# A two-block transformer kernel: state-space stage reordered, lag shifts on ScalarE's queue, E tables and a shared product on GpSimd

## The chip, the cores and the metric

The kernel runs on one core of a Trainium2 chip. The metric is the device time of one execution in microseconds, as the median of several; lower is better.

## The reference, cut to what matters

The input x is [512, 1024]. A first block has two layers: a state-space mixer (S5) and a latent attention, each followed by a SwiGLU feed-forward. A second block has two layers of three kinds of attention. The change touches only the S5 mixer:

```python
u = (h @ w_in).reshape(bsz, seq, SSM_GROUPS, SSM_GROUP)      # 64 groups of 16 channels
decay = exp(lam_re * step); a = decay * (cos(lam_im * step), sin(lam_im * step))   # 64 complex states a group
b = f(a) * (b_re, b_im)
x_t = a * x_(t-1) + b u_t;   y_t = Re(c x_t) + d_skip * u_t
z = gelu(y)
val, gate = split(z @ w_glu); out = val * sigmoid(gate)
```

## The kernel before

Every large product is exact in float32 by splitting both operands into a high and a low part (float32r): three matmuls for each 128x128 tile of weights. ScalarE makes the high part of a weight block (`wh`, line 645), VectorE the low part (`wl`, line 1203), two blocks ahead of TensorE (`split_high`, `split_low`, called through `ahead` and `next_block`). The blocks come in one stream over the whole kernel, through four slots of `raw` that SyncE's queue fills (`load`, line 411) once a slot has been split. All semaphores count upwards, so a count names a block or a turn.

**The state-space stage.** The sequence of 512 is cut into NCH = 64 chunks of CH = 8 steps. Inside a chunk the recurrence is a small lower triangular (Toeplitz) matrix over 8 steps; between chunks it is a scan. The 64 groups go through in NQ = 4 turns q of 16 groups (QP = 8 pairs). Tables come first: the powers of a (`pw`), the gained powers (`pf`), and E (`Er`, `Ei`, [128, 32 pairs, 64 chunks]), the phases of a^8 raised to the chunk's number, by doubling. Er and Ei are made on GpSimd up to 32 columns (lines 534 to 541). For the last doubling (columns 32 to 63) GpSimd makes Er (lines 546 to 548) and VectorE Ei (`last_phases`, line 1350).

For each turn q:

- `make_g(q)` (VectorE, five operations of 1024 columns): G, the input matrices. The first operation is the product `ps * br` into `tv`; it is used by two later ones.
- `from_g(q, hs)` (TensorE): transposes G into banks 4 and 5; `copy_w` (ScalarE) copies them to WM.
- `lags(q)` (TensorE, line 2030): the lag matrix of G and C; `copy_lags` (ScalarE, line 707) copies it to the last row block of MS; seven DMAs on SyncE's queue (`mat_shift`, line 451) shift it into the other seven. The rest of MS is zero from a GpSimd memset (line 558).
- `states(q)` (TensorE, line 2046): the input of the scan for each chunk, from U[q % 2] and WM. Its completion is z_made.
- VectorE rotates this by E (six operations), scans (line 1438, two scans, with the decay rows `rho` that ScalarE fills in `decay_rows`), rotates back and writes `state` (six operations): s_ready.
- `outputs(q)` (TensorE, line 2061): Toeplitz part from MS and U: toeplitz_used. `state_outputs(q)` (line 2072): adds the part of `state` through the V tables of `make_v(q)` (GpSimd, five operations of 1024 columns): y_ready.
- ScalarE applies Gelu (line 782), TensorE turns the result (`turn_z`, line 2082), ScalarE and VectorE write its high and low part to zH and zL (`turned_high`, line 760, `turned_low`, line 1417), the input of w_glu.

The order on TensorE is written out by hand. Eight products of w_in fill the first part (n = 0 to 7), with from_g(0) and lags(0) behind n = 4 and states(0) ahead of n = 7. Then from_g(1), lags(1), outputs(0), states(1), state_outputs(0); then a turn for q = 1, 2, 3 of from_g(q+1, first half), turn_z(q-1), from_g(q+1, second half), lags(q+1), outputs(q), states(q+1), state_outputs(q). In the last turn parts of the first two w_glu blocks (`glu_part`) stand in place of lags.

`take_input(j)` (VectorE, line 1375) scales product j of w_in into T; SyncE's queue writes it to u_dram (line 456) and reads it back in another layout to U (`read_u`, line 443, eight DMAs a turn). read_u(1) waits for the writes of all of u; read_u(2) and read_u(3) wait for y_ready(1) and (2), behind mat_shift of the turn.

The queues before: VectorE goes take_input(4), last_phases, take_input(5), block 5's split, make_g(1), take_input(6), block 6's split, take_input(7), then the turns q. In turn q it goes rotation, turned_low(q-1), scans, rotation back, state, make_g(q+2); behind q = 0's state also block 7's split (blocks 6 and 7 here are the splits made ahead for the first two w_glu blocks). GpSimd goes E, make_v(0), a wait for all of u, memsets of rho, state and MS, make_v(1), make_v(2) after y_ready(1), make_v(3). ScalarE goes splits, WM copies, a wait for the memsets, copy_lags(0), WM copies, decay_rows(0) and (1), then the turns.

## Time and profile before

| | |
|---|---|
| median of 3 runs | 1895.33 us (1894.39 to 1896.41) |
| profiled execution, its own time | 1895.86 us |
| span of its core, first to last instruction | 1894.1 us |
| mean granted clock of TensorE | 0.982 of 2.4 GHz |
| TensorE busy | 1825.6 us, 96% |
| VectorE, ScalarE, GpSimd busy | 1051.8, 834.4, 191.8 us |

PE is TensorE, PEld its weight loads, DVE VectorE, ACT ScalarE, POOL GpSimd, SPq SyncE's queue (DVEq: a semaphore increment on VectorE's queue). The span is the time between the first and the last instruction that the profiler recorded. Busy shares are averages over stages with different limits. The page's slices, of 47 us each, show where TensorE is not full:

```profile
PE   7789999999999999999999999989999999999997
DVE  8594454444433767766444434466464566555647
ACT  5132344344222666744444422233466633356753
POOL 7950000000000000000000000023000102200000
PEclk9779999999999999999999999999999999999999
```

Each digit is the busy share of one fortieth of the span in tenths; the last line is the granted clock of TensorE in tenths. The first four slices hold w_in and the state-space stage.

### The profile page before, as it was taken

The page shows a single profiled execution, that of the slowest core. Times are in us where ns is not written, and L with a number is a line of the kernel's source. Part 1 is how long each engine was busy: PE and PEld are TensorE (multiplying, and loading weights), DVE is VectorE, ACT ScalarE, POOL GpSimd, SP SyncE. Part 2 cuts the span into 40 slices and gives each one's busy share as a digit, 9 for nine tenths or more (in the row PEclk, how much of TensorE's full clock was granted, in tenths as well). Part 3 has the DMA queues.
Part 4 walks back from the last instruction along what each step waited for, and adds up shares of the span by engine and source line. Part 5 has one row for each costly group of instructions (what it writes and reads, how often), then busy time and mean ns, then how long its engine had stood idle before and what let it go on. Part 6 is the DMA issues. An engine that isn't in the chain of part 4 may idle for free.

```text
span 1894.1 us, 24279 instructions
## 1 busy us (share of the span) xinstructions
PE 1825.6 (96%) x8908; PEld 1415.8 (75%) x8908; DVE 1051.8 (56%) x1622; ACT 834.4 (44%) x1400; POOL 191.8 (10%) x261
## 2 busy tenths in 40 slices
PE   7789999999999999999999999989999999999997
PEld 5677878888888766667888888868766777866675
DVE  8594454444433767766444434466464566555647
ACT  5132344344222666744444422233466633356753
POOL 7950000000000000000000000023000102200000
PEclk9779999999999999999999999999999999999999
DMA  6212223222333210112322333323111122311111
GB/s 217 74 38 72 89 90 100 99 91 98 92 99 99 70 34 27 61 57 89 100 92 96 100 92 92 106 74 106 67 56 49 53 78 85 105 56 56 55 41 61
DMA packets 58763, 152.19 MB, mean 80 GB/s; under 512 B 17152, under 2 KB 22048, under 8 KB 58672
## 3 DMA queue, kind: packets, MB, share of 16 engines
q1 hardware_dynamic: 55120, 148.27, 24.5%
q0 software_dynamic: 3552, 2.70, 0.5%
q8 instruction: 58, 0.95, 0.2%
q14 instruction: 33, 0.27, 0.0%
HBM read 143.79 MB, written 4.19 MB: 78 GB/s over the span
## 4 chain that ended last, share of the span: by engine, by line
PE 86%; POOL 4%; DVE 3%; ACT 3%; issue 1%; SPq 1%; DMA 0%; DVEq 0%; ACTq 0%; POOLq 0%
PE bank L1974 18%; PE bank L1975 18%; PE bank L1976 18%; PE bank L2462 3%; PE bank L2464 3%; PE bank L2463 3%; PE bank L2439 2%; PE bank L2427 2%; PE bank L2426 2%; PE bank L2425 2%; PE bank L2194 1%; PE bank L2222 1%; PE bank L2549 1%; PE bank L2477 1%; PE bank L2446 1%
## 5 line engine op out<-in xcount | busy, mean ns | idle before, releaser
L1203 DVE TENSOR_TENSOR wl<-raw,wh 128x1024 fp32r<-128x1024 f32 (+3 forms) x280 | 323.6, 1156 | 495.1 <-ACT wh L645 492.0
L645 ACT ACTIVATE wh<-raw 128x1024 fp32r<-128x1024 f32 (+3 forms) x280 | 279.1, 997 | 592.8 <-PE bank L1976 516.8
L1974 PE MATMUL bank<-xH,wh 128*128 128x512 f32 x904 | 355.9, 394 | 12.5 <-DVE wl L1203 10.6
L1975 PE MATMUL bank<-xL,wh 128*128 128x512 f32 x904 | 353.1, 391 | 0.0
L1976 PE MATMUL bank<-xH,wl 128*128 128x512 f32 x904 | 353.0, 390 | 0.0
L1974 PEld LDWEIGHTS bank<-xH,wh 128*128 128x128 f32 x904 | 170.6, 189 | 51.1 <-DVE wl L1203 10.2
L1975 PEld LDWEIGHTS bank<-xL,wh 128*128 128x128 f32 x904 | 170.6, 189 | 35.8 <-issue 1.0
L1976 PEld LDWEIGHTS bank<-xH,wl 128*128 128x128 f32 x904 | 170.4, 188 | 35.8
L1974 PE MATMUL bank<-hidH,wh 128*128 128x512 f32 x352 | 137.4, 390 | 0.0
L1975 PE MATMUL bank<-hidL,wh 128*128 128x512 f32 x352 | 137.0, 389 | 0.0
L1976 PE MATMUL bank<-hidH,wl 128*128 128x512 f32 x352 | 137.0, 389 | 0.0
L2462 PE MATMUL bank<-xH,wh 128*128 128x512 f32 x256 | 108.4, 424 | 0.0
L2464 PE MATMUL bank<-xH,wl 128*128 128x512 f32 x256 | 100.8, 394 | 0.0
L2463 PE MATMUL bank<-xL,wh 128*128 128x512 f32 x256 | 100.3, 392 | 0.0
L581 POOL TENSOR_TENSOR xT<-xT,acc 128x512 f32<-128x512 f32 x9 | 11.2, 1272 | 737.0 <-ACT acc L1003 737.0
L1872 DVE TENSOR_REDUCE least<-bank 128x1 f32<-128x128 f32 (+3 forms) x96 | 42.6, 485 | 73.5 <-PE bank L2446 73.4
L1059 ACT ACTIVATE Pm<-bank,least 128x128 f32<-128x128 f32 (+3 forms) x96 | 49.8, 523 | 68.4 <-DVE least L1872 68.4
L1975 PEld LDWEIGHTS bank<-hidL,wh 128*128 128x128 f32 x352 | 66.1, 188 | 13.9 <-issue 0.2
L1974 PEld LDWEIGHTS bank<-hidH,wh 128*128 128x128 f32 x352 | 66.1, 188 | 13.9 <-issue 0.2
L1976 PEld LDWEIGHTS bank<-hidH,wl 128*128 128x128 f32 x352 | 66.1, 188 | 13.7
L811 ACT ACTIVATE hidH<-T 128x512 f32 (+1 forms) x44 | 27.8, 632 | 78.3 <-DVEq L1488 78.3
L571 POOL COPY xT<-T 128x512 f32<-128x512 f32 x8 | 8.9, 1107 | 475.8 <-DVE T L1506 475.8
(449 smaller groups left out, 3335.8 us busy)
## 6 DMA issues: line engine op xcount, KB each, us to landing
raw<-w_gu_dram SPq DMA_DIRECT2D x88, 512.0 KB, 3.3
raw<-w_p_dram SPq DMA_DIRECT2D x64, 512.0 KB, 3.3
raw<-w_dn_dram SPq DMA_DIRECT2D x32, 448.0 KB, 3.3
raw<-w_glu_dram SPq DMA_DIRECT2D x16, 512.0 KB, 3.6
raw<-w_dn_dram SPq DMA_DIRECT2D x16, 512.0 KB, 3.5
raw<-w_out_dram SPq DMA_DIRECT2D x16, 512.0 KB, 3.3
raw<-w_in_dram SPq DMA_DIRECT2D x8, 512.0 KB, 7.8
raw<-w_o_dram SPq DMA_DIRECT2D x8, 512.0 KB, 3.2
```

What stands on the lines that cost most here:

```text
L645: nc.scalar.activation(wh[:, (st.base + u) % 2, 0:kts * P], raw[:, (st.base + u) % 4, 0:kts * P], ACT.Copy).then_inc(w_high, 1)
L1059: nc.scalar.activation(Pm[side][:, POFF[j]:POFF[j] + w], banks[side][:, 0:w], ACT.Exp, scale=-1.0, bias=least[:, j, side:side + 1], accum_ ...
L1203: nc.vector.tensor_tensor(wl[:, s, 0:kts * P], raw[:, (st.base + u) % 4, 0:kts * P], wh[:, s, 0:kts * P].bitcast(F32), ALU.subtract).then_ ...
L1872: nc.vector.tensor_reduce(least[:, j, side:side + 1], banks[side][:, 0:(j + 1) * P], AX, ALU.min)\
L1974: nc.tensor.matmul(bank, wh[:, s, w], hi[:, k, :], start=first and kt == 0, stop=False)
L1975: nc.tensor.matmul(bank, wh[:, s, w], lo[:, k, :], start=False, stop=False)
L1976: ins = nc.tensor.matmul(bank, wl[:, s, w], hi[:, k, :], start=False, stop=last and kt == kts - 1)
L2425: nc.tensor.matmul(o, xH[:, k, rows], wh[:, s, w], start=k == 0, stop=False)
L2426: nc.tensor.matmul(o, xH[:, k, rows], wl[:, s, w], start=False, stop=False)
L2462: nc.tensor.matmul(bank, wh[:, s, w], xH[:, kt, :], start=kt == 0, stop=False)
L2463: nc.tensor.matmul(bank, wh[:, s, w], xL[:, kt, :], start=False, stop=False)
L2464: ins = nc.tensor.matmul(bank, wl[:, s, w], xH[:, kt, :], start=False, stop=kt == KD - 1)
```

## The change

- VectorE's `last_phases` is removed; GpSimd makes both Er and Ei of the last doubling.
- GpSimd makes the product `ps * br` of make_g for q = 2 and 3 (`make_t`), into two new buffers in the space of xH and xL, which is free only once w_in is done. make_t(2) stands behind make_v(0) and a wait for the last write of u, make_t(3) behind make_v(1).
- GpSimd's three memsets are removed: rho and state are now set on VectorE behind take_input(7) in turn 0, MS by an activation of ScalarE.
- The seven shift DMAs are issued by ScalarE's queue, in copy_lags. SyncE's queue issues read_u(q+2) once outputs(q) is done (toeplitz_used) and not after state_outputs(q).
- rotr and roti lie in `tv` now.
- ScalarE: behind block 6 the order is WM copies (0, 1) of q = 1, decay_rows(0), WM copies (2, 3), MS zeroed, copy_lags(0), decay_rows(1), block 7's split.
- VectorE: make_g(1) stands behind take_input(4), take_input(7) behind the rotation of turn 0; turned_low(q-1) behind the scans; the splits of blocks 6 and 7 behind turn 2's state.
- TensorE: five matmuls on a buffer of small constants before the first product; from_g(1, (0, 1)) and then states(0) ahead of n = 7, the other half behind it; lags(1) no longer waits for lag_ready(1).

```diff
--- before.py
+++ after.py
@@ -248,13 +248,13 @@
     pf = late.tensor("pf", [P, 3, CH, NPAIR])
     C2 = Region(nc, late.base + 4 * KB, 4 * KB).tensor("C2", [P, 2, 2, QP, 2, GK])
     core = Region(nc, shared.base, 32 * KB)
-    rotr = core.tensor("rotr", [P, QP, NCH])
-    roti = core.tensor("roti", [P, QP, NCH])
+    rotr, roti = (tv[:, ri * QP * NCH:(ri + 1) * QP * NCH].rearrange("p (a b) -> p a b", a=QP) for ri in range(2))
     rho = core.tensor("rho", [P, 2, QP, NCH])
     state = core.tensor("state", [P, 2, QP, NCH])
     zs = core.tensor("zs", [P, 2, CH, 4, GK])
     MS = core.tensor("MS", [P, CH, QG, GK])
     VM1 = [zL_mem.tensor("VM1r", [P, QP, P]), zH_mem.tensor("VM1i", [P, QP, P])]
+    shared_t = [core.tensor(f"shared_t{q}", [P, QP * CH * GK]) for q in range(2)]
     VM3 = [T[:, 2:4, :].rearrange("p a (b c) -> p (a b) c", c=P), core.tensor("VM3i", [P, QP, P])]
     skip_rows = zH_mem.tensor("skip_rows", [GK, NG, GK])
     U = [U0, u_mem.tensor("U1", [P, QG, NCH])]
@@ -444,13 +444,6 @@
                                  u_dram[q * QG:(q + 1) * QG, :, m, :].rearrange("g k c -> k g c"))\
                       .then_inc(sem(f"u_loaded{q % 2}"), 16)
 
-            def mat_shift(q):
-
-                sp.wait_ge(sem("lag_ready"), q + 1)
-                for l in range(CH - 1):
-                    sp.dma_start(MS[(CH - 1 - l) * GK:P, l, :, :], MS[0:(l + 1) * GK, CH - 1, :, :])\
-                      .then_inc(sem("shifted"), 16)
-
             for j in range(KD):
                 sp.wait_ge(sem("u_ready"), j + 1)
                 sp.dma_start(u_dram[j * 8:(j + 1) * 8].rearrange("g k m c -> (g k) (m c)"), T[:, j % 4, :])\
@@ -463,11 +456,9 @@
                 if j == 2 or j == 5:
                     load(stages["w_glu"], 0, j // 4 * 2)
                     load(stages["w_glu"], 0, j // 4 * 2 + 1)
-            for q in range(NQ):
-                mat_shift(q)
-                if q + 2 < NQ:
-                    sp.wait_ge(sem("y_ready"), q + 1)
-                    read_u(q + 2)
+            for q in range(NQ - 2):
+                sp.wait_ge(sem("toeplitz_used"), q + 1)
+                read_u(q + 2)
             st = stages["w_glu"]
 
             def rest_of_glu(i, last):
@@ -507,6 +498,14 @@
                 step(nc.gpsimd.tensor_tensor(v1, c_gap, pr, ALU.mult))
                 nc.gpsimd.tensor_tensor(v1, v1, t, ALU.subtract).then_inc(sem("v_ready"), 1)
 
+            def make_t(q):
+                pairs = slice(q * QP, (q + 1) * QP)
+                shape = [P, QP, CH, GK]
+                ps = pf[:, 2, :, pairs].rearrange("p l q -> p q l").unsqueeze(3).to_broadcast(shape)
+                br = Bz[:, 0, pairs, :].unsqueeze(2).to_broadcast(shape)
+                nc.gpsimd.tensor_tensor(shared_t[q - 2][:, :].rearrange("p (q l k) -> p q l k", q=QP, l=CH), ps, br, ALU.mult)\
+                  .then_inc(sem("t_ready"), 1)
+
             def v(name):
                 return sm[:, SM[name], :]
 
@@ -543,21 +542,17 @@
             wr, wi = (v(f"u1{c}").unsqueeze(2).to_broadcast([P, NPAIR, NCH // 2]) for c in "ri")
             low, high = slice(0, NCH // 2), slice(NCH // 2, NCH)
             t = tp[:, :].rearrange("p (a b) -> p a b", a=NPAIR)
-            step(nc.gpsimd.tensor_tensor(Er[:, :, high], Er[:, :, low], wr, ALU.mult))
-            step(nc.gpsimd.tensor_tensor(t, Ei[:, :, low], wi, ALU.mult))
-            step(nc.gpsimd.tensor_tensor(Er[:, :, high], Er[:, :, high], t, ALU.subtract))
+            cmul(Er[:, :, high], Ei[:, :, high], Er[:, :, low], Ei[:, :, low], wr, wi, t)
             pool.sem_inc(sem("phases_ready"), 1)
             pool.wait_ge(sem("powers_ready"), 1)
             pool.wait_ge(sem("sq_used"), KD)
             pool.wait_ge(sd_ready, 1)
             make_v(0)
+            pool.wait_ge(sem("u_written3"), 32)
+            make_t(2)
             pool.wait_ge(sem("v_ready"), 1)
-            pool.wait_ge(sem("u_ready"), KD)
-            step(nc.gpsimd.memset(rho[:, :, :, 0:1], 0.0))
-            step(nc.gpsimd.memset(state[:, :, :, 0:1], 0.0))
-            step(nc.gpsimd.memset(MS[:, :, :, :], 0.0))
-            pool.sem_inc(sem("pool_tables"), 1)
             make_v(1)
+            make_t(3)
             pool.wait_ge(sem("v_ready"), 2)
             pool.wait_ge(sem("y_ready"), 1)
             make_v(2)
@@ -706,6 +701,10 @@
                     act.wait_ge(sem("toeplitz_used"), q)
                 nc.scalar.activation(MS[:, CH - 1, :, :], lag_bank(q)[:, 0:QG * GK].rearrange("p (g k) -> p g k", g=QG), ACT.Copy)\
                   .then_inc(sem("lag_ready"), 1)
+                act.wait_ge(sem("lag_ready"), q + 1)
+                for l in range(CH - 1):
+                    act.dma_start(MS[(CH - 1 - l) * GK:P, l, :, :], MS[0:(l + 1) * GK, CH - 1, :, :])\
+                       .then_inc(sem("shifted"), 16)
 
             def lag_weights(q):
 
@@ -750,8 +749,6 @@
             next_block(5)
             lag_weights(1)
             next_block(6)
-            next_block(7)
-            copy_w(1, (0, 1))
 
             def turned_high(q):
                 for t in range(2):
@@ -759,12 +756,15 @@
                     act.wait_ge(sem("z_turned"), k + 1)
                     nc.scalar.activation(zH[:, k, :], z_bank(t)[:, :], ACT.Copy).then_inc(sem("z_high"), 1)
 
-            act.wait_ge(sem("pool_tables"), 2)
+            copy_w(1, (0, 1))
+            act.wait_ge(sem("phases_ready"), 1)
+            act.wait_ge(w_used, st.base + KD - 1 + 3)
+            decay_rows(0)
+            copy_w(1, (2, 3))
+            step(nc.scalar.activation(MS[:, :, :, :].rearrange("p l g k -> p (l g k)"), tiny[:, 2:3].to_broadcast([P, CH * QG * GK]), ACT.Copy))
             copy_lags(0)
-            copy_w(1, (2, 3))
-            act.wait_ge(sem("phases_ready"), 1)
-            decay_rows(0)
             decay_rows(1)
+            next_block(7)
             for q in range(NQ):
                 if q and q + 1 < NQ:
                     copy_w(q + 1, (0, 1))
@@ -1332,30 +1332,23 @@
                 pr, pi = (in_bank[:, ri, :, pairs].rearrange("p l q -> p q l").unsqueeze(3).to_broadcast(shape) for ri in range(2))
                 ps = pf[:, 2, :, pairs].rearrange("p l q -> p q l").unsqueeze(3).to_broadcast(shape)
                 br, b_sum, b_gap = (Bz[:, ri, pairs, :].unsqueeze(2).to_broadcast(shape) for ri in (0, 2, 3))
-                t = tv[:, :].rearrange("p (q l k) -> p q l k", q=QP, l=CH)
+                t = (tv if q < 2 else shared_t[q - 2])[:, :].rearrange("p (q l k) -> p q l k", q=QP, l=CH)
                 if 0 in parts:
-                    tt(t, ps, br, ALU.mult)
+                    if q < 2:
+                        tt(t, ps, br, ALU.mult)
                     if q:
                         dve.wait_ge(sem("lag_made"), q)
                         dve.wait_ge(sem("wt_ready"), 4 * q)
                     else:
                         dve.wait_ge(sem("pf_copied"), 1)
                     tt(G[:, 0], pi, b_sum, ALU.mult)
+                    if q >= 2:
+                        dve.wait_ge(sem("t_ready"), q - 1)
                     tt(G[:, 0], t, G[:, 0], ALU.subtract)
                 if 1 in parts:
                     tt(G[:, 1], pr, b_gap, ALU.mult)
                     tt(G[:, 1], G[:, 1], t, ALU.add)
                     dve.sem_inc(sem("g_ready"), 1)
-
-            def last_phases():
-
-                dve.wait_ge(sem("phases_ready"), 2)
-                wr, wi = (v(f"u1{c}").unsqueeze(2).to_broadcast([P, NPAIR, NCH // 2]) for c in "ri")
-                low, high = slice(0, NCH // 2), slice(NCH // 2, NCH)
-                t = tv[:, :].rearrange("p (a b) -> p a b", a=NPAIR)
-                tt(Ei[:, :, high], Er[:, :, low], wi, ALU.mult)
-                tt(t, Ei[:, :, low], wr, ALU.mult)
-                tt(Ei[:, :, high], Ei[:, :, high], t, ALU.add)
 
             dve.wait_ge(sem("vecs_loaded"), 16)
             st = stages["w_in"]
@@ -1402,13 +1395,10 @@
             take_input(3)
             next_block(4)
             take_input(4)
-            last_phases()
+            make_g(1)
             take_input(5)
             next_block(5)
-            make_g(1)
             take_input(6)
-            next_block(6)
-            take_input(7)
 
             def turned_low(q):
                 for t in range(2):
@@ -1430,13 +1420,17 @@
                 tt(zi, zi, ei, ALU.mult)
                 tt(zi, rotr[:, :, :], zi, ALU.add)
                 tt(zr, roti[:, :, :], zr, ALU.subtract)
-                if q:
-                    turned_low(q - 1)
+                if q == 0:
+                    take_input(KD - 1)
+                    step(nc.vector.memset(rho[:, :, :, 0:1], 0.0))
+                    step(nc.vector.memset(state[:, :, :, 0:1], 0.0))
                 dve.wait_ge(sem("rho_ready"), q + 1)
                 re, im = zi, zr
                 for r in (re, im):
                     step(nc.vector.tensor_tensor_scan(r.rearrange(flat), rho[:, q % 2, :, :].rearrange(flat),
                                                       r.rearrange(flat), 0.0, ALU.mult, ALU.add))
+                if q:
+                    turned_low(q - 1)
                 tt(rotr[:, :, :], re, er, ALU.mult)
                 tt(roti[:, :, :], im, er, ALU.mult)
                 tt(re, re, ei, ALU.mult)
@@ -1446,10 +1440,11 @@
                 tt(state[:, 0, :, 1:NCH], rotr[:, :, 0:NCH - 1], im[:, :, 0:NCH - 1], ALU.subtract)
                 tt(state[:, 1, :, 1:NCH], roti[:, :, 0:NCH - 1], re[:, :, 0:NCH - 1], ALU.add)
                 dve.sem_inc(sem("s_ready"), 1)
-                if q == 0:
-                    next_block(KD - 1)
                 if q + 2 < NQ:
                     make_g(q + 2)
+                elif q + 2 == NQ:
+                    next_block(KD - 2)
+                    next_block(KD - 1)
             turned_low(NQ - 1)
 
             st = stages["w_glu"]
@@ -2015,7 +2010,7 @@
 
             def lags(q):
 
-                if q:
+                if q >= 2:
                     pe.wait_ge(sem("lag_ready"), q)
                 elif q == 0:
                     pe.wait_ge(sem("mix_loaded"), 48)
@@ -2100,10 +2095,14 @@
                     ins.then_inc(w_used, 1)
 
             st = stages["w_in"]
+            pe.wait_ge(sem("tiny_ready"), 1)
+            for _ in range(5):
+                nc.tensor.matmul(banks[5][0:64, :], tiny[:, :], tiny[:, 2:3].to_broadcast([P, S]), start=True, stop=True)
             for n in range(KD):
                 if n:
                     pe.wait_ge(evicted, (2, 3, 4, 6, 7, 7, 8)[n - 1])
                     if n == 7:
+                        from_g(1, (0, 1))
                         states(0)
                     product(st, n // 4, n % 4, xH, xL, in_bank(n))
                 else:
@@ -2120,9 +2119,8 @@
                     from_g(0, (2, 3))
 
             st = stages["w_glu"]
-            from_g(1, (0, 1))
+            from_g(1, (2, 3))
             lags(1)
-            from_g(1, (2, 3))
             outputs(0)
             states(1)
             state_outputs(0)
```

## Rows read from the trace of the kernel before

**Rows 1.** Windows: stretch, length; busy (count) of PE, PEld, DVE, ACT, POOL; clock; DMA; GB/s.

```profile
0.00:178.08 178.08, 144.56 (x1352) 122.66 (x1353) 129.19 (x179) 54.72 (x94) 105.40 (x114) 0.88 0.30 98
178.08:1894.10 1716.02, 1681.03 (x7556) 1293.14 (x7556) 922.58 (x1443) 779.64 (x1306) 86.39 (x147) 0.99 0.25 79
```

**Rows 2.** Waits of TensorE in the first 220 us (total, times, longest).

```profile
PE bank L2025 <- ACT MS L707: 6.7, 1, 6.7
...
PE bank L2061 <- DMA MS<-MS: 3.4, 2, 1.8
...
PE bank L2072 <- DVEq L1448: 0.6, 1, 0.6
```

**Rows 3.** Chain of waits, on GpSimd before the lag copy (start, length, what).

```profile
83.60 1.81 POOL MS L558
```

**Rows 4.** Timeline of TensorE in the state-space stage (start, length, instructions, idle before).

```profile
66.39 2.10 PE L2046 MATMUL bank<-U,WM 128*64 128x64 f32 x64 [0.95 <-DVEq L1376]
...
95.80 3.68 PE L2061 MATMUL bank<-MS,U 128*64 128x128 f32 x32
104.16 3.71 PE L2046 MATMUL bank<-U,WM 128*64 128x64 f32 x64 [4.67 <-DVEq L1448]
...
123.27 3.68 PE L2061 MATMUL bank<-MS,U 128*64 128x128 f32 x32 [1.83 <-DMA MS<-MS]
126.71 2.20 PE L2046 MATMUL bank<-U,WM 128*64 128x64 f32 x64
...
133.32 1.09 PE L2013 MATMUL bank<-cons,G 128*128 128x128 f32 x8 [0.76 <-DVEq L1348]
...
149.62 3.71 PE L2072 MATMUL bank<-VM,state 64*64 64x128 f32 x64
```

**Rows 5.** Windows of the first 150 us, all engines (columns as in rows 1).

```profile
9.72:14.17 4.45, 4.44 (x11) 3.47 (x12) 4.39 (x7) 4.45 (x7) 3.80 (x8) 1.00 1.02 415
14.17:18.60 4.43, 4.43 (x20) 3.64 (x19) 3.95 (x16) 2.58 (x5) 3.65 (x11) 1.00 1.04 385
58.60:67.70 9.10, 8.15 (x76) 6.67 (x76) 8.75 (x5) 3.02 (x6) 8.90 (x3) 1.00 0.06 21
...
85.55:96.70 11.15, 10.78 (x50) 9.79 (x52) 0.68 (x1) 1.71 (x4) 10.74 (x5) 0.50 0.33 81
81.85:86.25 4.40, 0.33 (x1) 0.33 (x2) 4.17 (x6) 0.38 (x1) 4.04 (x5) 0.50 0.33 100
126.95:133.20 6.25, 5.61 (x129) 5.29 (x125) 6.13 (x4) 0.98 (x3) 6.09 (x3) 1.00 0.01 3
133.35:145.80 12.45, 10.83 (x128) 10.00 (x130) 11.96 (x16) 4.31 (x8) 4.12 (x2) 0.79 0.33 81
112.40:121.45 9.05, 9.04 (x116) 8.14 (x114) 8.74 (x12) 5.85 (x13) 8.47 (x5) 0.93 0.37 87
```

**Rows 6.** Timeline of VectorE.

```profile
36.58 1.30 DVE L1203 TENSOR_TENSOR wl<-raw,wh 128x1024 fp32r<-128x1024 f32 x1 [1.09 <-ACT wh L645]
...
80.90 0.68 DVE L1375 TENSOR_TENSOR T<-bank,R 128x512 f32<-128x512 f32 x1
```

**Rows 7.** Timeline of GpSimd, two steps of one doubling.

```profile
39.97 0.63 POOL L515 TENSOR_TENSOR tp<-Ei,sm 128x256 f32<-128x256 f32 x1
40.68 1.61 POOL L516 TENSOR_TENSOR Er<-Er,tp 128x256 f32<-128x256 f32 x1
```

**Rows 8.** Timeline of SyncE's queue, the reads of U for q=1.

```profile
83.88 3.76 SPq L443 DMA_DIRECT2D U<-u_dram  x8
```

**Rows 9.** DMA issues of the first 170 us (KB each, median us to landing).

```profile
U<-u_dram SPq DMA_DIRECT2D x32, 64.0 KB, 2.4
...
MS<-MS SPq DMA_DIRECT2D x4, 112.0 KB, 2.2
```

**Rows 10.** Timeline of ScalarE, two copies to WM.

```profile
78.82 1.08 ACT L699 ACTIVATE WM<-bank 128x512 f32<-128x512 f32 x2 [3.07 <-PE bank L2013]
```

**Rows 11.** Line 451, the shift DMAs on SyncE's queue (ns min/median/max).

```profile
L451 SPq DMA_DIRECT2D MS<-MS x28: 529/593/1052, 87.7 to 152.5; - x28
```

## The prediction

> **What bounds the kernel now.** I first cut the span in two [rows 1]. After 178 us TensorE is busy 1681 of 1716 us at clock 0.99: that part is a stream of weight products, the change does not touch it, and it moves earlier by whatever the first part gives up. In the first 178 us TensorE is busy only 145 us, at clock 0.88. This is where the change works.
>
> Next, the waits of TensorE there [rows 2]: 6.7 us until ScalarE has copied the lag matrix to MS, 3.4 us (twice) for the DMAs that shift MS, 0.6 us for VectorE's last states. The chain of waits [rows 3] tells what ScalarE's copy waited for: GpSimd's memset of MS, ending at 85.4, which stands in GpSimd's queue behind its V tables for q=0. The TensorE timeline [rows 4] adds a wait of 4.7 us for VectorE's states before states(1) at 104.2 and 0.8 us before the transposes at 133.3. It also shows what idling costs: states(0) took 2.1 us, states(1) after the wait 3.7. So until about 104 us the stage is a latency chain over five engines, and after it TensorE's own work with small holes.
>
> **First rounds of w_in.** TensorE issued 11 matmuls in the first 4.45 us, 20 in the next 4.43 [rows 5]: it began at the lower level, 1.2 GHz. Five warm-up matmuls on idle time can save up to 2.1 us there. VectorE's table work runs unbroken meanwhile, so little of this passes through: its split at 36.6 waited 1.1 us for ScalarE [rows 6], which waited for a product. That product now ends earlier, but ScalarE must first copy pf, so I take 0.9 us; bounds 0 and 1.1. No row shows the warm-up matmuls; if they stayed cold they might delay the first product by about 1 us. Neither value changes the sum below, because the chain in which they stand has 1.2 us of slack.
>
> **VectorE and GpSimd before the scans.** VectorE no longer makes half of the last E doubling, for whose start it had to wait for GpSimd. make_g(1) now fills that wait and ends before product 6 does. So TensorE finds G(1) ready. Product 6 ended 0.95 before states(0) began at 66.4, at 65.4; now 64.5. from_g(1,(0,1)) takes 1.1, states(0) 2.1 [rows 4], and 24 matmuls at 0.23 (20 in 4.43 [rows 5]) 5.5: product 7 ends at 73.2.
>
> GpSimd now does six operations for the last doubling, not three. Its chain does not depend on TensorE; the doubling started at 58.6. Operations of this size took 11.15 us for five when VectorE left GpSimd alone, 9.1 us for three when both worked [rows 5]: 13.4 us for six at best, 18.2 at worst. The window now holds only one split of VectorE, so I take 13.4. But make_g(1) and that split put four VectorE operations with two SBUF inputs into GpSimd's path from 48 us on; where such an operation met a GpSimd one, that took 1.61 us against 0.63 for its neighbour of the same size [rows 7], so about 0.9 each, 3.6 us. E is ready at 58.6+3.6+13.4 = **75.6** (bounds 72.0 and 80.4).
>
> The Trainium skill (SBUF — State Buffer, Who interferes with whom) says that a VectorE instruction with two SBUF inputs and a GpSimd one that reads SBUF exclude each other for the whole instruction. By that alone the four would cost their full length, about 5.0 us for 3.6, and the time would be 1.4 us higher.
>
> **What waits behind phases_ready 3.** VectorE now waits for the whole E before the rotation, and take_input(7), formerly ahead of it, is queued behind. Rotation 4.4 us [rows 5]: 80.0; take_input(7): 80.9, against 81.6 before [rows 6]. From it hang the write of the last part of u and the eight reads of U[1]: issued 83.9 to 87.6 before [rows 8], landing 2.4 us later [rows 9], 90.0; now **89.3**. The scans no longer wait for rho. A whole turn from rotation to states is 12.45 us [rows 5]; less the rotation, and less turned_low's two subtractions (about 0.65 each, as the operation of 512 columns in [rows 6]), scans and states are 6.8. With two memsets (0.3) s_ready(1) comes at 88.0 (104.0 before).
>
> **MS on ScalarE.** After product 7 (73.2): decay_rows(0); from_g(1,(2,3)) to 74.4; two copies, 1.1 us [rows 10], 75.5. Zeroing MS is one activation of 2048 columns. No row has that; below lies 1.1 us (a split of 1024 columns), above four copies of 512, 2.2; scaling gives 2.0: 77.5. Lag copy 0.4. Then seven DMA issues. No DMA of ScalarE's queue is in the trace; SyncE's same issues took 0.53 to 1.05 us, median 0.59 [rows 11], and the largest landed 2.2 us later [rows 9]. I take 0.6: landed at 84.4. lags(1) no longer waits for MS and ends near 79, so TensorE idles over 5 us and starts outputs(0) cold, 3.7 us [rows 4]: 84.4 to 88.1.
>
> **The sum.** states(1) starts at the latest of 88.1 (outputs(0)), 88.0 (states) and 89.3 (U[1]). Before, it started at 104.2. It and state_outputs(0) then took 8.4 us, most of it cold. In the next turn the clock was back after a cold outputs(1): states(2) took 2.2, and a warm state_outputs 3.7 [rows 4]. I take 5.8 (bounds 5.8 and 8.4), so y_ready(1) at 95.1 instead of 112.45: **17.35 us**. GpSimd's v(0) (86.8) and shared product (89) come in time.
>
> q=1: issued by ScalarE right after outputs(q), beside the U reads, the shifts land some 9 us before outputs(q+1): 1.8 us. q=2: 1.6 and the 0.8 before the transposes. q=3: the 0.6. Together **4.8**. For this three covers must hold. VectorE's turn is now 6.25 (make_g without its first product) + 12.45 [rows 5] = 18.8 us against TensorE's 18.5 (9.05 of transposes, turned z and lags [rows 5], 3.7, 5.8), so its states, ready at 88.0, 106.8, 125.6, stand only 1.0 and 0.7 us ahead of TensorE. ScalarE has 5.8 us between toeplitz_used and y_ready for 0.4 of copy and 4.2 of issues before the Gelu is due. The two w_glu splits moved behind q=2 on VectorE (1.3 us each, as the split in [rows 6]) put its last states at 125.6+2.6+12.45 = 140.7; TensorE wants them about 10 us after y_ready(3) at 131.9 (Gelu, turned z, 24 matmuls of w_glu, outputs), at 142. read_u goes from y_ready to toeplitz_used, early enough. GpSimd's removed memsets (2 us) lie on no path any more.
>
> 17.35+4.8 = 22.15. The profiled execution took 1895.9 us, span 1894.1 and 1.8 around it, 0.5 above the median of 1895.33. From the median: **1873.1 us**. It can be better by little: with E at 72.0 the MS chain holds (1.2 more), with issues of 0.53 us 0.5 more, and with the clock up during outputs(1) and (2) VectorE, 1.0 and 0.7 behind, allows 1.7: 1870.
>
> **Rivals.** (B) *GpSimd becomes the bound.* Work moves to the engine that two-input VectorE operations slow: 9.1 us for three says that six may take 18.2. Then U[1] lands at 94.1: 1877.9, and with a cold pair (2.6) 1880.5. For it: the old doubling ran at that rate. Against: its heaviest partners, VectorE's own half, are gone.
>
> (C) *The clock stays down.* For it: the first part has 0.88 against 0.99 in the rest [rows 1], and without a long product between 79 and 131 us the stage may never recover: states and state_outputs at twice the warm 5.8 less a little (3.7+7.4), three times, +15.9: 1889. Against it: after 3.7 us of cold outputs at 123.3, states(2) ran at the quick rate [rows 4].
>
> (D) *Slower: ScalarE's queue.* If an issue there holds the queue until it lands (2.1 us), four sets of seven stand in front of outputs(0) and of three Gelus. The first set has 1.2 us of slack beyond its 4.2, the others 5.3 each: the cost at p us per issue is 28p−21.3, which passes the gain of 22.2 at p=1.55; at 2.1 it is 37.5 and the time 1910.6. For it: an issue of SyncE took as much as 1.05. Against: its median is 0.59 although landings take 2.2, so the queue does not wait there.
>
> (E) *The change does not do what it says:* a cover fails from the first turn on (shared product or V late, G late), which gives the holes back: 1890 to 1896.
>
> **Chances.** My forecast, 1870 to 1876: 0.64. B, 1876 to 1882: 0.23. C: 0.05. D: 0.04. E: 0.04. The range 1870 to 1882 leaves the last three out. A measurement can tell 0.2%, 3.8 us. Faster: forecast, B, and C, 0.93 with a part of E; same 0.03; slower 0.04.
>
> **What the changed profile would show.** The first w_in matmul at 9.7 with 0.23 us between starts; phases complete near 75.6; take_input(7) near 80.9; six MS-side operations on ScalarE from 73 to 78 and seven issues of 0.6; outputs(0) at 84.4, cold; states(1) at 89.3; ends of state_outputs at 95, 113, 132, 146; no wait of outputs for a DMA; everything after 178 shifted as a block. I am wrong if ScalarE's issues cost over 1 us, if E comes after 80, if the Gelus start late after y_ready, or if VectorE's states hold states(2) and (3).

## The result, and the profile after

The changed kernel took 1874.34 us in the median of 4 runs (1873.54 to 1875.42), the kernel before, run beside it, 1895.09 us (4 runs, 1894.39 to 1896.41). The ratio is 0.989 [0.9873, 0.9907]: 20.75 us gained, 22.2 forecast. The profiled execution took 1874.83 us with a span of 1873.0, 0.5 above its median, as the one before was. Of the executions of the kernel before that ran beside the experiments, one took 4531.31 us; it is left out of the ratios.

First the cut of the span, as in [rows 1], then the stretches that answer to [rows 5]. Columns: stretch, length; busy time (count) of PE, PEld, DVE, ACT, POOL; granted clock; DMA share; GB/s.

```profile
0.00:158.44 158.44, 142.54 (x1362) 117.84 (x1363) 116.89 (x176) 56.13 (x95) 111.45 (x116) 0.91 0.38 110
158.44:1873.00 1714.56, 1679.68 (x7556) 1292.00 (x7556) 922.61 (x1443) 779.68 (x1306) 86.38 (x147) 0.99 0.25 79
9.52:13.97 4.45, 4.45 (x19) 3.67 (x20) 4.30 (x7) 4.45 (x8) 3.80 (x8) 1.00 1.02 410
60.51:75.02 14.51, 14.51 (x124) 12.24 (x123) 4.96 (x4) 4.11 (x8) 14.07 (x6) 1.00 0.32 109
81.70:88.80 7.10, 0.00 (x0) 0.03 (x1) 6.64 (x9) 2.47 (x6) 6.94 (x5) 0.50 1.00 141
97.65:115.40 17.75, 16.00 (x277) 14.92 (x276) 15.77 (x18) 7.41 (x15) 17.36 (x8) 1.00 0.29 65
115.40:134.40 19.00, 19.00 (x274) 17.90 (x274) 16.97 (x21) 5.33 (x10) 11.45 (x6) 0.82 0.36 90
```

The rest of the program is the same 7556 matmuls and starts at 158.44 instead of 178.08: 19.64 us of the 21.1 between the two spans came out of the first part. The last 1.46 lie in the untouched rest (1714.56 against 1716.02); counted from the end of the last outputs, that rest takes 1723.8 to 1726.5 us in the profiles of this study, so they can't be put down to the change. The first products of w_in now begin quick (19 matmuls in 4.45 us, 11 before). The rows print a clock of 1.00 for both, so that the lower level before is read from the spacing of the matmuls alone (0.43 us against 0.23). From 81.70 to 88.80 TensorE does nothing. It stood still for 6.7 us before too, in its wait for the lag copy; what is new is that the DMA engines are busy all the time (share 1.00).

The waits of TensorE in the first 200 us:

```profile
PE bank L2056 <- DMA MS<-MS: 7.1, 1, 7.1
PE bank L2077 <- ACT zs L782: 2.4, 2, 1.7
...
PE bank L2008 <- DVEq L1351: 1.8, 1, 1.8
```

Against [rows 2], the 6.7 us for the lag copy, the two later waits for the shift DMAs and the one for VectorE's last states are gone, and so are the 4.7 us before states(1) [rows 4]. One wait of 7.1 us is left, at outputs(0), and two are new: 1.7 us at the transposes of turn 0, for ScalarE's Gelu, and 1.8 us for G(0). The timeline of TensorE shows where they stand (compare [rows 4]):

```profile
45.79 1.09 PE L2008 MATMUL bank<-cons,G 128*128 128x128 f32 x8 [1.76 <-DVEq L1351]
...
47.47 7.04 PE L2025 MATMUL bank<-C,G 128*128 128x32 f32 x32
...
76.30 1.03 PE L2008 MATMUL bank<-cons,G 128*128 128x128 f32 x8
...
88.80 3.37 PE L2056 MATMUL bank<-MS,U 128*64 128x128 f32 x32 [7.12 <-DMA MS<-MS]
91.99 2.09 PE L2041 MATMUL bank<-U,WM 128*64 128x64 f32 x64
94.01 3.71 PE L2067 MATMUL bank<-VM,state 64*64 64x128 f32 x64
...
100.49 2.08 PE L2077 MATMUL bank<-cons,zs 64*64 64x64 f32 x64 [1.75 <-ACT zs L782]
...
107.84 1.97 PE L2056 MATMUL bank<-MS,U 128*64 128x128 f32 x32
```

The outputs of turn 0 end at 97.65, those of the others at 115.40, 134.4 and 148.5 (before 112.45, 132.6, 153.4, 168.05). So 14.8 of the 19.6 us are there by the end of turn 0, and 4.75 come in turns 1 to 3.

What 88.80 waits for is read from the chain of waits:

```profile
80.40 0.62 ACTq L706
...
84.27 4.40 DMA MS<-MS
...
94.54 2.03 ACTq L706
```

GpSimd's memset [rows 3] has left the chain. ScalarE's queue stands in it twice: with the shifts of turn 0, whose last takes 4.4 us to land, and with those of turn 1, behind which the Gelu is queued. ScalarE's own timeline:

```profile
78.05 1.91 ACT L764 ACTIVATE MS<-tiny 128x2048 f32<-128x2048 f32 x1
...
80.40 4.49 ACTq L706 DMA_DIRECT2D MS<-MS  x7
...
92.69 5.83 ACTq L706 DMA_DIRECT2D MS<-MS  x7
98.55 1.28 ACT L782 ACT_TABLE_LOAD   x1 [5.89 <-issue]
99.84 1.08 ACT L782 ACTIVATE zs<-bank 128x512 f32<-128x512 f32 x2
```

VectorE gets E from GpSimd at 75.06, which ends a wait of 6.48 us, and rotates; take_input(7) follows:

```profile
75.06 1.42 DVE L1243 TENSOR_TENSOR tv<-bank,Er 128x512 f32<-128x512 f32 x2 [6.48 <-POOLq L546]
...
79.44 0.69 DVE L1368 TENSOR_TENSOR T<-bank,R 128x512 f32<-128x512 f32 x1
...
86.12 1.39 DVE L1243 TENSOR_TENSOR state<-tv,bank 128x504 f32<-128x504 f32 x2
```

### The profile page after: what moved, and what is told of

The parts are those of the page before. It is cut to its first block, busy times and chain, and to the rows that moved or that the text cites. A ratio compares the mean times of both kernels' runs of the same rounds, so it can differ in the third digit from the quotient of the medians.

```text
span 1873.0 us, 24302 instructions
## 1 busy us (share of the span) xinstructions
PE 1822.2 (97%) x8918; PEld 1409.8 (75%) x8918; DVE 1039.5 (55%) x1619; ACT 835.8 (45%) x1401; POOL 197.8 (11%) x263
## 4 chain that ended last, share of the span: by engine, by line
PE 90%; DVE 4%; ACT 3%; issue 1%; DMA 1%; ACTq 1%; SPq 0%; POOL 0%; DVEq 0%
PE bank L1969 19%; PE bank L1970 18%; PE bank L1971 18%; PE bank L2460 3%; PE bank L2462 3%; PE bank L2461 3%; PE bank L2437 2%; PE bank L2423 2%; PE bank L2425 2%; PE bank L2424 2%; PE bank L2192 1%; PE bank L2220 1%; PE bank L2547 1%; DVE wl L1203 1%; PE bank L2475 1%
## 5 line engine op out<-in xcount | busy, mean ns | idle before, releaser
L1867 DVE TENSOR_REDUCE least<-bank 128x1 f32<-128x128 f32 (+3 forms) x96 | 42.6, 485 | 73.5 <-PE bank L2444 73.4
```

The costliest lines, as they stand in the source:

```text
L1867: nc.vector.tensor_reduce(least[:, j, side:side + 1], banks[side][:, 0:(j + 1) * P], AX, ALU.min)\
```

## The experiments

Up to the start of turn 0 the trace left the forecast in two places: product 7's end (76.3, not 73.2) and the shifts' landing (4.4 us, not 2.2). Theory 1 takes them as what sets the start of turn 0: TensorE reached G(0) early, waited 1.76 us and ran lags(0) slowly (7.04 us; 3.76 before), and the shifts share the DMA engines with SyncE's reads of U[1]. The rival: three chains end within 1 to 3 us of each other at states(1) (the shifts, the reads of U[1], VectorE's states), so that a faster one only uncovers the next. The change's other parts were then undone one at a time. Medians of the kernel before beside these runs: 1895.83 (runs 1 to 4), 1895.07 (5 to 8) and 1895.03 (9 to 12). The ratios differ from the quotients of these medians by up to 0.0006. An interval is some 3 us wide on either side, so differences of a few us can only rest on the traces, or on ranges that do not overlap. Each kernel has one profile, of one execution.

### 1. The changed kernel again

> The changed kernel once more, for its spread. In its first profile lags(0) ran at the lower clock (7.04 us for 32 matmuls against 3.76 in the kernel before), behind a wait of 1.8 us for G(0). Theory 1: the early arrival at that wait causes the drop, so it comes again: 7.0 us, and the time is 1874.3 within 1 us. Rival: the drop falls there by chance, and lags(0) shows 3.8 us in this profile.

1875.46 us (1874.81 to 1877.5), ratio 0.9898 [0.9882, 0.9914]. The same picture: a wait of 1.95 us for G(0), lags(0) in 7.04, outputs(0) at 89.3, last outputs ended at 149.4. Both late steps came again here. They do not come in every execution, though: up to product 7 the code of runs 3, 4, 6, 7, 9 and 12 below is that of the changed kernel, and over these eight profiles lags(0) takes 3.76 to 7.04 us and product 7 ends anywhere from 70.9 (run 3) to 79.3 (run 7).

### 2. No warm-up

```diff
-            pe.wait_ge(sem("tiny_ready"), 1)
-            for _ in range(5):
-                nc.tensor.matmul(banks[5][0:64, :], tiny[:, :], tiny[:, 2:3].to_broadcast([P, S]), start=True, stop=True)
```

> The five matmuls ahead of the first product are taken out. Theory 1: w_in starts at the lower clock again and comes 2.1 us later, TensorE then finds G(0) almost ready, lags(0) stays at about 3.8 us, and product 7 ends near 74.5 instead of 76.3. The MS chain hangs from it, so the time falls by 1 to 2 us against the changed kernel: 1872.5 to 1873.5. Rival (the warm-up is worth its 0.9 us or has no effect): 1874.3 to 1875.3, product 7 at 76 to 77.

1874.18 us (1872.9 to 1874.92), ratio 0.9889 [0.9873, 0.9905]. TensorE came to G(0) 2.5 us later, hardly waited, and ran lags(0) at the quick rate:

```profile
47.23 1.09 PE L2008 MATMUL bank<-cons,G 128*128 128x128 f32 x8 [0.69 <-DVEq L1351]
...
48.87 3.76 PE L2025 MATMUL bank<-C,G 128*128 128x32 f32 x32
...
85.70 3.68 PE L2056 MATMUL bank<-MS,U 128*64 128x128 f32 x32 [5.83 <-DMA MS<-MS]
```

The windows of the two lags(0), first the changed kernel's, then this one's (columns as above), show the clock: 0.50 of full speed, 1.2 GHz, after the wait of 1.76 us, 0.99 here.

```profile
47.47:54.50 7.03, 7.03 (x34) 7.03 (x34) 2.34 (x3) 0.10 (x1) 6.48 (x8) 0.50 0.21 82
```

```profile
48.87:52.60 3.73, 3.73 (x34) 3.73 (x34) 2.37 (x3) 0.13 (x1) 3.57 (x3) 0.99 0.37 141
```

Product 7 ended at 74.5, the last shift landed 3.1 us after its issue and not 4.4, outputs(0) began 3.1 us earlier, and then states(3) waited 1.0 us for VectorE, until 126.3. The first product of w_glu came at 156.1, 2.3 us earlier. In time 1.3 us are left against run 1, less than an interval can tell. So, against the changed kernel's profile, the warm-up's 2 us at the start were paid back at lags(0). Product 7's end alone would not show it: without a warm-up it came at 74.5, 75.7 and 73.5 (runs 2, 10, 11), inside the 70.9 to 79.3 with one. In time the warm-up is worth nothing that can be told.

### 3. The table of the Gelu loaded ahead of the shifts of turn 1

```diff
+                if q == 0:
+                    nc.scalar.preload_act_table(ACT.Gelu_apprx_tanh)
                 if q + 1 < NQ:
```

> ScalarE loads the Gelu table while it waits for outputs(0), ahead of copy_lags(1), and not behind the seven issues. Theory 1: the Gelu of turn 0 comes 1.3 us earlier and TensorE's wait of 1.7 us for it nearly goes: 1872.8 to 1873.4. Rival: TensorE's wait was set by the issues alone, or VectorE's states hold the next states anyway: no change, 1874.3.

1875.22 us (1874.36 to 1876.04), ratio 0.9892 [0.9877, 0.9908]: no gain, though the wait for turn 0's Gelu is gone and this execution, in which nothing ahead of the shifts of turn 0 was edited, also ran lags(0) at the quick rate (3.76 us after a wait of 0.99) and had outputs(0) at 81.3. Its waits of TensorE between 60 and 160 us tell why:

```profile
PE bank L2058 <- DMA MS<-MS: 4.8, 1, 4.8
PE bank L2043 <- DMA U<-u_dram: 4.5, 1, 4.5
PE bank L2043 <- DVEq L1444: 2.5, 2, 2.3
```

With the shifts 7.5 us earlier (the last lands 2.3 us after its issue, ahead of the reads), states(1) waits 4.5 us for U[1], until 89.4, and later states(3) waits 2.3 us for VectorE, until 126.5. The second half of the rival holds: other chains decide.

### 4. The shifts back on SyncE's queue

```diff
             for q in range(NQ):
+                sp.wait_ge(sem("lag_ready"), q + 1)
+                for l in range(CH - 1):
+                    sp.dma_start(MS[(CH - 1 - l) * GK:P, l, :, :], MS[0:(l + 1) * GK, CH - 1, :, :])\
+                      .then_inc(sem("shifted"), 16)
                 if q + 2 < NQ:
+                    sp.wait_ge(sem("y_ready"), q + 1)
                     read_u(q + 2)
...
-                    act.dma_start(MS[(CH - 1 - l) * GK:P, l, :, :], MS[0:(l + 1) * GK, CH - 1, :, :])\
```

> The shift DMAs go back to SyncE's queue, with read_u(q+2) behind y_ready as in the kernel before; all else as changed. Theory 1: shift 0 is issued behind the eight reads of U, from 86 to 91, and lands near 93 instead of 88.7; the waits of outputs(1) and (2) for the shifts come back (1.8 and 1.6 us), the late Gelu (1.7) goes: 5 to 8 us slower than the changed kernel, 1879 to 1882. Rival (the two streams share the DMA engines, so who issues hardly matters): within 2 us of it.

1883.51 us (5 runs, 1881.44 to 1884.43), ratio 0.9935 [0.9921, 0.9949]: 8 to 9 us slower than the changed kernel, more than expected. Waits of TensorE and SyncE's queue:

```profile
PE bank L2057 <- DMA MS<-MS: 18.0, 3, 11.4
```

```profile
82.05 3.76 SPq L443 DMA_DIRECT2D U<-u_dram  x8
85.85 4.41 SPq L462 DMA_DIRECT2D MS<-MS  x7
```

On the one queue the shifts of turn 0 stand behind the eight reads of U[1], although their data are ready at 79.3; outputs(0) starts at 92.0. Outputs(1) and (2) wait again, 3.9 and 2.6 us. This is the largest part of the change, and it is an order, not a rate: seven issues take as long on either queue (4.41 us here, 4.49 on ScalarE's for turn 0). With the shifts, the reads of turns 2 and 3 went back behind the end of state_outputs; the run does not tell the two apart.

### 5. The wait for G(0) filled with matmuls of constants

```diff
                 if n == 4:
+                    for _ in range(2):
+                        nc.tensor.matmul(banks[5][0:64, :], tiny[:, :], tiny[:, 2:3].to_broadcast([P, S]), start=True, stop=True)
                     from_g(0, (0, 1))
```

> The changed kernel with two more matmuls on the constants (0.86 us each at the upper clock) just before from_g(0,(0,1)), where TensorE waits 1.8 us for G(0). Theory 1 (the wait lets the clock fall in lags(0)): lags(0) takes 3.8 us and not 7.0, product 7 ends near 73, the shifts are issued before the reads of U[1] and land 2.2 us after issue; then U[1], near 89, decides: 1 to 2 us faster than the changed kernel. Rival (the light matmuls of from_g and lags bring the clock down by themselves): lags(0) still 7.0 us, no change or 0.5 us slower.

```profile
44.12 1.94 PE L2118 MATMUL bank<-tiny 128*64 128x512 f32 x4
45.99 1.09 PE L2008 MATMUL bank<-cons,G 128*128 128x128 f32 x8
...
47.64 3.76 PE L2025 MATMUL bank<-C,G 128*128 128x32 f32 x32
```

With the wait filled, from_g and lags(0) start within 0.2 us of where they start in the changed kernel, and lags(0) takes 3.76 us instead of 7.04; product 7 ends at 73.3, the 73.2 of the forecast. Yet the time is 1874.36 us (1873.8 to 1875.56), ratio 0.989 [0.9875, 0.9905]: nothing, where 1 to 2 us were expected. States(1) waits for U[1] until 89.5 and states(3) 2.3 us for VectorE. The slow lags(0) cost 3 us of its own chain, and almost nothing of the time. The rival is not quite refuted either: with no wait left, the granted clock still falls to 0.50, from 52 to 54 us, right behind the same light matmuls. It falls there in run 2 too (0.63 in these 2 us), and not in runs 3 and 11 (1.00). So the wait moves the fall forward, into lags(0); it does not alone cause it.

### 6. The low parts of z ahead of the scans again

```diff
+                if q:
+                    turned_low(q - 1)
                 dve.wait_ge(sem("rho_ready"), q + 1)
...
-                if q:
-                    turned_low(q - 1)
                 tt(rotr[:, :, :], re, er, ALU.mult)
```

> VectorE writes the low parts of z ahead of the scans again, as in the kernel before; all else as changed. Theory 1 (VectorE's chain of states stands only 1 to 2 us ahead of TensorE): in turn 1 the scans wait for ScalarE's high parts, s_ready(2) comes 2.5 us later, TensorE waits about 1 us for it and again in turn 2: 1 to 2.5 us slower than the changed kernel. Rival (TensorE and the Gelu decide in these turns): no change.

1877.32 us (1875.27 to 1880.44), ratio 0.9911 [0.9896, 0.9926], 2 to 3 us slower in the median; but its times overlap those of the changed kernel (1873.54 to 1877.5), and so do the intervals, so this is not shown. The scans of turn 1 begin at 100.5 (98.9 in the changed kernel), with the rotation ended at the same time. In its one profile (span 1874.3) the waits for states that this should bring are only 0.6 us; where the rest of the time goes the trace does not show.

### 7. The shared product back on VectorE

```diff
-            make_t(2)
             pool.wait_ge(sem("v_ready"), 1)
             make_v(1)
-            make_t(3)
...
-                    if q < 2:
-                        tt(t, ps, br, ALU.mult)
+                    tt(t, ps, br, ALU.mult)
```

> The shared product of make_g for turns 2 and 3 goes back to VectorE, GpSimd makes none. Theory 1: 1.25 to 2.7 us more on VectorE in two turns against 1.5 us of slack, so states(2) and states(3) wait: 1 to 3 us slower than the changed kernel. Rival (the wait for GpSimd's product costs VectorE as much as it saves): no change.

1879.12 us (5 runs, 1877.25 to 1879.43), ratio 0.9913 [0.9899, 0.9926], 4 to 5 us slower in the median, with ranges that overlap by a little (1877.25 the lowest here, 1877.5 the highest there). The product itself now stands in VectorE's turn:

```profile
109.78 3.08 DVE L1241 TENSOR_TENSOR tv<-pf,Bz 128x1024 f32<-128x1024 f32 x1
```

But from the end of turn 0 to the end of turn 3 this profile has 51.8 us against 50.85. The other 2.9 us of its later end were lost earlier (a wait of 2.19 us for G(0), lags(0) in 7.0, product 7 ended at 79.3 instead of 76.3), in a part that the edit does not touch and that scatters by as much between executions (run 1). About 1 us is located; the rest is open.

### 8. Half of the last E doubling back on VectorE, after make_g(1)

```diff
             make_g(1)
+            last_phases()
             take_input(5)
```

with last_phases() making Ei of the upper half in three operations, as before the change, and GpSimd only the three of Er.

> VectorE makes the Ei half of the last doubling again, behind make_g(1); GpSimd only Er. Theory 1: E is ready near 70 and not at 75, U[1] could come 4 us earlier, but take_input(5), the next split and product 7 come 5 us later on VectorE's account, and the MS chain that hangs from product 7 decides: 2 to 4 us slower. Rival (E decides the start of states(1)): 2 to 4 us faster.

1881.42 us in the median of 5, but from 1873.12 to 1884.77, ratio 0.9934 [0.992, 0.9947]. The profile is of the 1873.12 execution: the rotation starts 3.2 us earlier, at 71.9, states(0) waits 1.1 us for VectorE and outputs(0) starts at 87.8. It shows nothing of the 8 us by which the median lies above it. What the other four executions did is not known, and this run settles nothing but that the place is a bad one: four of its five times lie above all of the changed kernel's. It can't tell what E alone is worth.

### 9. MS zeroed by GpSimd again

```diff
+            step(nc.gpsimd.memset(MS[:, :, :, :], 0.0))
+            pool.sem_inc(sem("pool_tables"), 1)
             make_t(2)
...
-            step(nc.scalar.activation(MS[:, :, :, :].rearrange("p l g k -> p (l g k)"), tiny[:, 2:3].to_broadcast([P, CH * QG * GK]), ACT.Copy))
+            act.wait_ge(sem("pool_tables"), 2)
```

> MS is zeroed by GpSimd again, behind make_v(0) and ahead of make_t(2); ScalarE waits for it before copy_lags(0); all else as changed. Theory 1 (taking MS out of GpSimd's queue is a main part of the gain): make_v(0) ends near 86, the memset near 88, the shifts land near 95 and not at 88.7: outputs(0) 6 us later, 5 to 7 us slower than the changed kernel, 1880 to 1882. Rival (U[1], the states and the lags hold the start anyway): within 2 us of it.

1881.49 us (5 runs, 1880.18 to 1882.41), ratio 0.9929 [0.9915, 0.9943], 6 to 7 us slower, as expected. Outputs(0) waits 10.8 us for the shifts. GpSimd's timeline:

```profile
85.97 1.80 POOL L553 MEMSET MS<- 128x2048 f32 x1
```

The memset is quicker than ScalarE's activation (1.80 against 1.91 us); it is late because GpSimd is behind V for q=0.

### 10. No warm-up, MS zeroed and shifted ahead of the second copies to WM, table early

```diff
             decay_rows(0)
-            copy_w(1, (2, 3))
             step(nc.scalar.activation(MS[:, :, :, :].rearrange("p l g k -> p (l g k)"), tiny[:, 2:3].to_broadcast([P, CH * QG * GK]), ACT.Copy))
             copy_lags(0)
+            copy_w(1, (2, 3))
```

and the edits of 2 and 3.

> No warm-up; ScalarE zeroes MS, copies the lags and issues the shifts ahead of the WM copies (2, 3) of turn 1; the Gelu table is loaded ahead of copy_lags(1). Theory 1 (VectorE's chain of states, which starts with E at 75, decides from turn 2 on): outputs(0) starts 1.1 us earlier than without the warm-up alone (84.6) and the wait for the first Gelu (0.7) goes, but states(3) still starts near 126.3: 1873 to 1874.3, at most 1 us faster than without the warm-up alone. Rival (the MS chain decides): 1.5 to 2 us faster than that, 1872.5 or less.

1873.77 us (1873.34 to 1875.07), ratio 0.9887 [0.9871, 0.9903]. Outputs(0) starts at 85.9 and not at the 84.6 expected, as product 7 ended at 75.7. States(1) starts at 89.3, 2.7 us earlier than in the changed kernel, and states(3) then waits 1.1 us for VectorE until 126.5: the same floor as in runs 2, 3 and 5 (126.3 to 126.5). VectorE's states begin with the rotation, and that with E.

### 11. The same, and half of the last E doubling on VectorE where it is idle

```diff
             next_block(5)
+            last_phases()
             take_input(6)
```

> As r10, and VectorE makes the Ei half of the last doubling, behind the split of block 5, so that it delays neither take_input(5) nor that split. Theory 1: E is ready near 70.5, s_ready(1) near 84 and not 87.5, VectorE no longer decides, and the MS chain gives states(1) at 88 to 89: 1.5 to 3 us faster than r10, 1870.5 to 1872.5. Rival (GpSimd and VectorE slow each other, take_input(6) and product 7's followers come later): no faster than r10.

**1870.95 us** (4 runs, 1869.84 to 1871.74), ratio 0.9872 [0.9856, 0.9888]. Its first part:

```profile
0.00:154.30 154.30, 136.80 (x1352) 116.22 (x1353) 123.18 (x179) 56.16 (x95) 108.07 (x113) 0.93 0.37 113
```

TensorE waits 4.3 us for the shifts of turn 0. The rotation starts at 72.3 and VectorE's states are ready 2.8 us earlier (84.7 against 87.5); no state is waited for any more, turns end at 93.4, 111.0, 130.2 and 144.4, and w_glu starts at 154.3. All its times lie below all 8 of the changed kernel (1873.54 to 1877.5, runs of 1 included): 3.4 us below the changed kernel's median, 4.5 below that of run 1, and the best version here. Beside run 10, from which it differs by the one edit, it is 2.8 us faster, again with ranges apart. Between the two profiles the last outputs end 3.5 us earlier. Some 2 of these were there at product 7 (73.5 against 75.7), ahead of the place of the edit, and are within that product's scatter. What E gave is a lower floor: states(3) starts at 123.6, where four runs could not start it before 126.3. E was ready at 72.3, not at the 70.5 expected. Freeing the shifts (10) gave nothing that can be told, and E on top of it did. The E half at this place without the edits of run 10 was not tried; run 8 had it at another.

### 12. The reads of U[1] behind the shifts of turn 0

```diff
+                    if j == 7:
+                        sp.wait_ge(sem("shifted"), 16 * (CH - 1))
                     read_u(j // 7)
```

> The changed kernel, but SyncE's queue waits until the first seven shifts have landed before it issues the reads of U[1]. Theory 1 (shifts and reads of U in flight together double each other's time to landing): the last shift lands 2.2 us after its issue and not 4.4, outputs(0) starts 2 us earlier (86.6), but U[1] lands near 93 to 94 and holds states(1): 1 to 2.5 us slower. Rival (the 4.4 us come from ScalarE's queue itself): still 4.4 us to landing, outputs(0) at 88.8.

1877.98 us (5 runs, 1876.46 to 1879.16), ratio 0.9911 [0.9897, 0.9925], 2.5 to 3.6 us slower in the median (its lowest time, 1876.46, lies below the changed kernel's highest). First the DMA issues of the changed kernel between 80 and 90 us, then of this one between 79 and 85 (KB each, median us to landing):

```profile
U<-u_dram SPq DMA_DIRECT2D x8, 64.0 KB, 4.4
...
MS<-MS ACTq DMA_DIRECT2D x1, 112.0 KB, 4.4
```

```profile
MS<-MS ACTq DMA_DIRECT2D x1, 112.0 KB, 2.3
```

Alone, the largest shift lands in 2.3 us; beside the reads it takes 4.4, and the reads take 4.4 too, 2.4 before [rows 9]. The other profiles agree: 2.3 in run 3, whose shifts were issued ahead of the reads, 2.2 in run 4 behind them, 3.1 in runs 2, 8 and 10, where the two overlap in part, 4.5 in run 1. But the reads, issued from 85.9, now hold states(1) until 92.5. So the contention is real and costs the shifts 2.1 us, and giving either transfer precedence takes more from the other. The Trainium skill (DMA: Bandwidth & Descriptors, Issuing engines are not separate DMA queues) says that transfers issued by different engines run on the same 16 DMA engines and interleave; the DMA share of 1.00 from 81.7 to 88.8 and these landings agree.

## Why the prediction held, and where its steps failed

The time (1874.3) lies in the likeliest case, 1.2 us above the 1873.1. That it came so near is in part luck: the first part gave 2.5 us less than the 22.15 of the sum (19.64), and the untouched rest gave 1.46 that no term had. Point by point:

**Start of turn 0.** Forecast: y_ready(1) at 95.1, 17.35 us earlier. Measured: 97.65, 14.8 us. States(1) was to start at the latest of three, and the mechanism held, but not the order: U[1] was named (89.3), the shift chain was it (outputs(0) from 88.8, states(1) at 91.99). The failed step is the shift chain's 84.4, which came 4.4 us late. Three terms of it were mis-sized, by the changed kernel's profile:

- *Product 7 ends at 73.2*: 76.3, 3.1 late. The forecast gave the warm-up a slack of 1.2 us to vanish in and no price. With it TensorE waited 1.76 us for G(0), and lags(0) ran at 1.2 GHz, 3.3 us longer than before. Runs 2 and 5 show this link from both sides: arrive later, or fill the wait, and lags(0) takes 3.76 us. It is a tendency and no certainty, as run 3 shows with the same code (70.9); a forecast of one value for this step could not have held.
- *The landing of 2.2 us* [rows 9]: 4.4, as the reads of U[1] were in flight. That landing was taken from a kernel in which both transfers stood on one queue; moved to another, they overlap. Run 12 isolates it: 2.3 alone.
- *Everything between* came 1.0 us sooner than forecast; 0.6 of it is that a landing counts from the start of its issue, while the forecast put it behind the issue's end. The zeroing took 1.91 for the 2.0 estimated, an issue 0.62 for 0.6.

That only 2.55 of the 4.4 us reached y_ready(1) is because U[1] would have held states(1) until about 89.4 in any case, as runs 3 and 5 show: there lags(0) was quick and the shifts landed before U[1], and nothing measurable was gained. After their waits for U[1] states(1) and state_outputs(0) took 7.2 us, not the 5.7 of the changed kernel.

**E.** Forecast 75.6, measured 75.0, and by its own terms. The four two-input operations of VectorE each met one of GpSimd, which took 0.77 to 1.08 us longer than it does alone: 3.7 us in all, where 3.6 were taken. The six operations of the last doubling took 14.5 us, 12.9 without the two meetings that fell in them, where 13.4 were taken. The two in question, GpSimd's first and third operation, with what VectorE ran beside them:

```profile
60.51 2.69 POOL L513 TENSOR_TENSOR Er<-Er,sm 128x1024 f32<-128x1024 f32 x1 [0.18 <-POOL sm L518]
...
65.27 3.26 POOL L515 TENSOR_TENSOR Er<-Er,tp 128x1024 f32<-128x1024 f32 x1
```

```profile
60.19 1.23 DVE L1243 TENSOR_TENSOR G<-G,tv 128x1024 f32<-128x1024 f32 x1
...
63.59 2.67 DVE L1203 TENSOR_TENSOR wl<-raw,wh 128x1024 fp32r<-128x1024 f32 x1 [0.46 <-ACT wh L640]
```

The first VectorE operation ends at 61.42, 0.91 us after GpSimd's began, and GpSimd's takes 0.77 longer than the 1.92 of its like; the split ends at 66.26, 0.99 after GpSimd's third began, which takes 0.87 longer than the 2.39 of its like. The other two meetings give 1.08 for 1.22 and 0.96 for 1.10. So GpSimd lost, within 0.15 us, what was left of VectorE's operation when its own began, and not that operation's full length. By the full length, as the forecast read the Trainium skill (SBUF — State Buffer, Who interferes with whom), E would have come at 77.0. The trace agrees with the exclusion that the page states, and not with the 5.0 us that the forecast worked out from it. Take_input(7) began at 79.4 and ended at 80.1 (80.9 forecast), VectorE's states were ready at 87.5 (88.0). Rival B had its condition, GpSimd slowed, but the doubling took 14.5 us and not 18.2.

**Turns 1 to 3.** Forecast 4.8 us, measured 4.75, but not by its own sum. The Gelu of turn 0 was to fit: 5.8 us for 0.4 and 4.2. What it met was 5.83 us of issues, one of them 2.03, and the table load of 1.28 us, which the forecast did not have. TensorE waited 1.75 us. Against that, outputs(1) ran in 1.97 us, where outputs(1) before took 3.68; the forecast kept the cold figure. The covers for q=2 and q=3 held: no wait for shifts, none for states.

**VectorE's chain** was put 1.0 and 0.7 us ahead of TensorE. It never shows in the changed kernel, because TensorE itself is 2.55 us late. In runs 2, 3, 5 and 10, where it is not, states(3) is held at 126.3 to 126.5 for 1.0 to 2.3 us. That is why these runs gain so little, and why 11, which moves E, does.

**Rival D**, ScalarE's queue: p was 0.62, far from its break-even of 1.55, with one issue of 28 at 2.03 us. **Rival C**, the clock staying down: the turns had 1.00 and 0.82, and cost what was forecast. **Rival E**: no cover of the shared product or of V failed.

**Slips in its arithmetic**, none of which matters: 6.25+12.45 is 18.7 and not 18.8, 1895.33 less 22.15 is 1873.2 and not 1873.1.

**What the parts are worth**, each undone alone, by medians against 1874.3 to 1875.5: the shifts on ScalarE's queue 8 to 9 us, MS zeroed by ScalarE 6 to 7, the shared product 4 to 5 measured (1 located), the scans ahead of the low parts 2 to 3, the warm-up nothing. Only the first two stand clear of the spread; the third is at its edge, the fourth lies in it. The forecast's one sum gave none of these separately; its largest items, the memset out of GpSimd's queue and the shifts next to their data, are the two largest. Not settled: what makes product 7's end scatter from 70.9 to 79.3, the spread of run 8, the place of 3 us in run 7 and of 2 in run 6.

## What to carry to other kernels

Where several chains meet at one instruction, write down the arrival of each; the gain of shortening one is the distance to the next, and an edit that gains nothing may only have uncovered the next chain (run 10, then run 11). Where a step scatters between executions, one profile does not show what an edit did to it. A transfer moved to another queue is no longer ordered behind its neighbours but overlaps with them: take its landing from a stretch where both run, not from the old order. Let an engine arrive early only where something is ready for it: here 2 us gained at the start of w_in went in the light matmuls behind the wait they opened.

## What the runs showed of the hardware that was not expected

Waits of only 1.76 to 2.2 us were followed, in six profiles of six, by slow light matmuls; in the changed kernel's the granted clock was 0.50 there. Over 14 profiles the wait for G(0) and the duration of the 32 matmuls of lags(0) after it were:

```text
wait for G(0), us    lags(0), us
0 to 0.4             3.8                (before, run 5, run 11)
0.6 to 1.0           3.8, 3.8, 4.4, 5.0, 6.3   (runs 2, 3, 10, 6, 12)
1.76 to 2.2          5.1, 5.8, 7.0 four times  (runs 4, 8; after, 1, 7, 9)
```

The longer waits go with the slower lags(0), but it is no function of the wait alone: from 0.6 to 1.0 us, both rates occur, and with no wait the clock fell right behind lags(0) (run 5).

An issue on ScalarE's queue took 0.54 to 2.03 us:

```profile
L706 ACTq DMA_DIRECT2D MS<-MS x28: 537/617/2034, 80.4 to 133.1; - x28
```

against 0.53 to 1.05 on SyncE's [rows 11]. The one long issue ran while the DMA engines were 0.47 busy; the issue ahead of it took 0.61 us at 0.76. So their load alone does not explain it, and its cause is open. It is no accident of one execution: in each of the eleven other profiles with the shifts on ScalarE's queue the longest issue took 1.31 to 1.80 us, while with the shifts back on SyncE's queue (run 4) it took 0.60.
